# Two-block model: projection of block 2 by token tiles, one router for both tiles, softmax division on GpSimd, output stored in quarters

## What is computed

```python
def second_block(x, mem, g_mix, w_in, qk_gain, na_rpb, t5_table, g_mem, w_mem_kv, w_out, g_ffn, w_r1, b_r1, w_r2, b_r2, w1, w3, w2):
    ...
        x = x + jnp.concatenate([out_na, out_dil, out_mem], axis=-1) @ w_out[l]
        x = x + hierarchical_moe(rms_norm_2(x, g_ffn[l]), w_r1[l], b_r1[l], w_r2[l], b_r2[l], w1[l], w3[l], w2[l])

def hierarchical_moe(h, w_r1, b_r1, w_r2, b_r2, w1, w3, w2):
    ...
    grp_logits = (t @ w_r1).astype(jnp.float32) + b_r1.astype(jnp.float32)
    grp_prob = jax.nn.softmax(grp_logits, axis=-1)
    grp_idx = jnp.argmax(grp_logits, axis=-1)
    ...
    fine_logits = ((t @ w_r2).astype(jnp.float32) + b_r2.astype(jnp.float32)).reshape(n, N_GROUPS, EXPERTS_PER_GROUP)
    fine_sel = jnp.take_along_axis(fine_logits, grp_idx[:, None, None], axis=1)[:, 0]
    top_val, top_idx = lax.top_k(fine_sel, TOP_K)
    gate = grp_gate * jax.nn.softmax(top_val, axis=-1)
    ...
        a = jax.nn.silu(xb @ w1[e]) * (xb @ w3[e])
        return a @ w2[e]
```

## Time and profile before

| | us |
|---|---|
| runs of the kernel | 2553.66, 2555.37, 2559.77 (median 2555.37) |
| the profiled execution, whole | 2554.65 |
| its span in the profile | 2552.9 |
| PE / DVE / ACT / POOL busy | 2091.7 / 1346.4 / 846.9 / 622.0 |
| attention of block 2 | from 1945.8 to 2016.3 |
| output projection, norm, router | from 2016.4 to 2083.0 |
| rounds of experts | from 2083.0 to 2544.9 |
| output store | from 2546.5 to the end |

### The profile page before, as it was taken

The page is one execution under the profiler, slowest core; times in us unless marked ns, Lnnn a source line. Parts: engine busy times, 40 slices in busy tenths (PEclk is TensorE's granted clock), DMA queues, the critical chain, the costliest instruction groups (busy, mean ns, idle before and its releaser), DMA issues.

```text
span 2552.9 us, 24815 instructions
## 1 busy us (share of the span) xinstructions
PE 2091.7 (82%) x8226; PEld 1068.0 (42%) x8226; DVE 1346.4 (53%) x3202; ACT 846.9 (33%) x2245; POOL 622.0 (24%) x585
## 2 busy tenths in 40 slices
PE   5997978798799889799889779877999966666665
PEld 1554632354264455265456224322674532222221
DVE  2885887666647966646976577764106230111110
ACT  1214144344436644435734344443104210000000
POOL 1000044433334433333433444442101000000000
PEclk9997999999999999999999999999999978888888
DMA  8792799999999999999999999999540139999997
GB/s 331 296 372 89 296 374 421 421 421 420 394 421 421 388 417 421 421 397 421 365 410 422 421 421 418 414 421 418 197 160 34 67 147 428 427 429 428 428 429 325
DMA packets 107145, 915.96 MB, mean 359 GB/s; under 512 B 12406, under 2 KB 12692, under 8 KB 15572
## 3 DMA queue, kind: packets, MB, share of 16 engines
q0 software_dynamic: 76800, 549.70, 52.8%
q1 hardware_dynamic: 30228, 364.82, 34.5%
HBM read 913.37 MB, written 6.06 MB: 360 GB/s over the span
## 4 chain that ended last, share of the span: by engine, by line
PE 39%; DMA 36%; DVE 15%; ACT 6%; issue 3%; POOL 1%; SPq 0%; DVEq 0%; POOLq 0%; ACTq 0%
DMA arena<-in_peer_uv_dram,arena 18%; PE summed L1071 15%; DMA arena<-in_moe_pieces_dram 15%; PE gp L1143 5%; DVE y L2224 4%; PE gp L873 3%; DMA arena<-in_w_slots_dram 3%; PE gp L858 3%; DVE h L2026 2%; PE gp L1139 2%; PE gp L1404 2%; PE turned L958 1%; ACT arena L1652 1%; PE scores L944 1%; ACT L1646 1%
## 5 line engine op out<-in xcount | busy, mean ns | idle before, releaser
L1071 PE MATMUL summed<-arena 128*128 128x512 f32 x2048 | 993.5, 620 | 210.8 <-ACT arena L1652 187.6
L2224 DVE CUSTOM_DVE_ANT_0 y<-arena,h 128x1024 f32<-128x1024 f32 x512 | 627.2, 1225 | 398.7 <-DMA arena<-in_peer_uv_dram,arena 351.5
L804 POOL DMA_INDIRECT arena<-in_peer_uv_dram,arena x512 | 580.2, 1133 | 925.2 <-PE summed L1071 809.1
L1071 PEld LDWEIGHTS summed<-arena 128*128 128x128 f32 x2048 | 367.5, 193 | 749.1 <-ACT arena L1652 403.9
L1646 ACT ACTIVATE arena<-arena 128x1 f32<-128x1 f32 x512 | 102.8, 201 | 517.6 <-DVE arena L2224 517.0
L1404 PE MATMUL gp<-arena,mod 128*32 128x512 f32 x1024 | 161.2, 764 | 120.7 <-DMA arena<-in_moe_pieces_dram 119.5
L1652 ACT ACTIVATE arena<-cst,arena 128x128 f32<-128x128 f32 x512 | 205.8, 402 | 16.7
L2554 DVE TENSOR_TENSOR mod<-mod,gp 128x512 f32<-128x512 f32 x8 | 5.5, 689 | 385.4 <-ACT mod L1876 385.4
L1649 ACT ACTIVATE arena<-arena 128x1 f32<-128x1 f32 x512 | 151.1, 295 | 20.8 <-DVE arena L2213 4.1
L873 PE MATMUL gp<-hT,arena 128*128 128x256 f32 x608 | 135.6, 386 | 4.1 <-DMA arena<-in_w_slots_dram 3.3
L1404 PEld LDWEIGHTS gp<-arena,mod 128*32 128x32 f32 x1024 | 31.9, 125 | 245.0 <-DMA arena<-in_moe_pieces_dram 184.1
(11 more groups left out here) (399 smaller groups left out, 2033.7 us busy)
## 6 DMA issues: line engine op xcount, KB each, us to landing
arena<-in_moe_pieces_dram SPq DMA_DIRECT2D x96, 2048.0 KB, 25.7
arena<-in_w_slots_dram SPq DMA_DIRECT2D x47, 2048.0 KB, 10.0
mod<-in_w_parts_dram SPq DMA_DIRECT2D x29, 1024.0 KB, 9.3
arena<-in_w_parts_dram SPq DMA_DIRECT2D x29, 1024.0 KB
arena<-in_peer_uv_dram,arena POOLq DMA_INDIRECT x512
t_rep<-t_rows POOLq DMA_DIRECT2D x1, 3066.0 KB, 14.8
arena<-t_rep POOLq DMA_DIRECT2D x1, 2304.0 KB, 11.1
na_rep<-na_rows POOLq DMA_DIRECT2D x1, 1778.0 KB, 7.7
```

Of the source, the lines that this page charges most:

```text
L804: pool.indirect_dma_start(rowbuf[b], None, a["peer_uv"].rearrange("l n d -> (l n) d"), bass.IndirectOffsetOnAxis(ap=idx[:, col(n):col(n) + ...
L1071: mm = pe.matmul(op[:, b, :], diag[:, n % DIAGS, :], rowbuf[n % ROWS][:, D + b * 512:D + (b + 1) * 512], start=n % SLOTS == 0, stop=n % SL ...
L2224: v.tensor_tensor_reduce(y[:, t, :], rowbuf[n % ROWS][:, 0:D], h[:, t, :], 1.0, 0.0, ALU.mult, ALU.add, dots[:, c:c + 1]).then_inc(udot, 1)
```

## The change

POOL no longer builds diagonal matrices. It multiplies each segment's exponentials, in place, by the inverse sums (128x512 in block 2; in MoBA 128x128 and 128x256), and PE transposes them with the identity. PE now waits per segment, not per unit. The projection goes tile 0 of both slots, then tile 1. Residual, norm, transposition and router product are done per tile, and the filling multiplications are gone. The router treats both tiles in one instruction where it can; `r_done` is raised once `picked` is there, and the gates follow while PE makes the ranks. The count of overflowing tokens comes after the first `select`, and PE waits for `flag_ready` only after the first `up`. The last `scatter` uses four PSUM banks. Each quarter of `x` is stored when its last addition is done, ahead of the branch.

```diff
-        in_order += phase_slots["in2"] + phase_slots["out2"]
+        in_order += phase_slots["in2"]
         order += [(n, j) for n in in_order for j in range(len(slots[n][2]))]
+        order += [(n, t) for t in range(T) for n in phase_slots["out2"]]
...
+            for n in range(2 * T):
+                c = slice(n % 2 * CH, (n % 2 + 1) * CH)
+                sync.wait_ge(scat_read, 4 * (QUADS - 1) + n + 1)
+                sync.dma_start(out[0, n // 2 * P:(n // 2 + 1) * P, c], x[:, n // 2, c]).then_inc(out_done, 16)
             sync.wait_ge(flag_ready, 1)
...
+            def divide_rows(stage_name):
+
+                units, segs = att[stage_name]
+                u0 = unit_base[stage_name]
+                for i, sg in enumerate(segs):
+                    u = sg["u"]
+                    if sg["first"]:
+                        pool.wait_ge(d_inv, u0 + u + 1)
+                    inv = den[:, 2 * (u % 4):2 * (u % 4) + 2]
+                    if sg["keys"][0] == S:
+                        c0 = CH * (i % 6 % 3)
+                        rows = logits[stage_name][i % 6 // 3][:, c0:c0 + CH].rearrange("p (t n) -> p t n", t=T)
+                        pool.tensor_tensor(rows, rows, inv.unsqueeze(2).to_broadcast([P, T, S]), ALU.mult).then_inc(scale_ready, 1)
+                    else:
+                        for t in range(T):
+                            rows = logit(stage_name, sg, i, t)
+                            ins = pool.tensor_tensor(rows, rows, inv[:, t:t + 1].to_broadcast([P, sg["keys"][t]]), ALU.mult)
+                        ins.then_inc(scale_ready, 1)
...
-                    pe.wait_ge(scale_ready, u0 + sg["u"] + 1)
+                    pe.wait_ge(scale_ready, b0 + i + 1)
...
-                                mm = pe.matmul(tp[:, i % 2, c * S + t * P:c * S + (t + 1) * P],
-                                               logit(stage_name, sg, i, t)[:, c * P:(c + 1) * P], scale[:, t, :], start=True, stop=True)
+                                mm = pe.transpose(tp[:, i % 2, c * S + t * P:c * S + (t + 1) * P],
+                                                  logit(stage_name, sg, i, t)[:, c * P:(c + 1) * P], ident)
...
-            project("out2")
-            keep_clock("out2", 8)
-            turn_h(4)
-            hT_ready()
-
             for t in range(T):
+                project("out2", tile=t)
+            for t in range(T):
+                pe.wait_ge(h_ready, 4 * T + t + 1)
+                turn_rows(h[:, t, :])
+                hT_ready()
...
-            pe.wait_ge(flag_ready, 1)
...
             up(0)
+            pe.wait_ge(flag_ready, 1)
             turn_sel(0, False)
...
-            residual("out2", T * 5)
-            norm(4, x)
+            for t in range(T):
+                v.wait_ge(gemm_moved, group_of[phase_slots["out2"][-1], t] + 1)
+                v.tensor_tensor(x[:, t, :], x[:, t, :], y[:, t, :], ALU.add).then_inc(x_ready, 1)
+                v.wait_ge(x_ready, 4 * T + t + 1)
+                sum_of_squares(t)
+                last_norm(t)
```

More of the change, by code:

```diff
@@ L817, in _ @@
             load_gain(5, a["g_ffn_2"][0])
[L818 removed]
+            divide_rows("block2")
         @block.tensor
@@ L1853, in _ @@
             attention("block2")
-            move("out2")
-            norm(4)
-            move_turned()
+            move("out2", tile=0)
+            tile_root(4 + 2 * T)
+            move("out2", tile=1)
+            move_turned_rows(0)
+            tile_root(4 + 2 * T + 1)
+            move_turned_rows(1)
             act.wait_ge(r_pre, 1)
-            act.activation(route[:, 128:136], route[:, 128:136], ACT.Exp).then_inc(r_exp, 1)
-            act.wait_ge(r_pre, 2)
-            act.activation(route[:, 136:138], route[:, 136:138], ACT.Exp).then_inc(r_exp, 1)
+            act.activation(route[:, 128:138], route[:, 128:138], ACT.Exp).then_inc(r_exp, 1)
             def expert(e2, i):
@@ L1992, in attention @@
                             if u >= 4:
-                                v.wait_ge(scale_ready, u0 + u - 3)
+                                v.wait_ge(scale_ready, b0 + units[u - 4]["first"] + units[u - 4]["n"])
                             if stage_name == "moba":
@@ L2127, in rms_heads @@
                 link(v.reciprocal(small[:, c1:c1 + T * nh], small[:, c1:c1 + T * nh]))
-            def residual(name, n):
-                v.wait_ge(gemm_moved, last_group[name])
-                for t in range(T):
-                    v.tensor_tensor(x[:, t, :], x[:, t, :], y[:, t, :], ALU.add).then_inc(x_ready, 1)
-                v.wait_ge(x_ready, n)
             def first_residual(t):
@@ L2522, in _ @@
-            v.sem_inc(r_done, 1)
+                ins = v.max(gm[:, t, :], gl8[:, t, :])
+            link(ins)
+            for t in range(T):
+                ins = v.max_index(route_u[:, 8 * t:8 * t + 8], gm[:, t, :], gl8[:, t, :])
+            link(ins)
+            link(v.tensor_copy(gi.unsqueeze(2), route_u[:, 0:16].rearrange("p (t n) -> p t n", t=T)[:, :, 0:1]))
+            v.tensor_tensor(ge, gl8[:, :, 0:4], gm[:, :, 0:1].to_broadcast([P, T, 4]), ALU.subtract)
+            link(v.tensor_tensor(oh, iota[:, 0:4].unsqueeze(1).to_broadcast([P, T, 4]), gi.unsqueeze(2).to_broadcast([P, T, 4]), ALU.is_equal))
@@ new lines, in _ @@
+            for t in range(T):
+                ins = v.tensor_tensor(tmp[:, t], fine[:, t, :].rearrange("p (g n) -> p g n", g=N_GRP),
+                                      oh[:, t, :].unsqueeze(2).to_broadcast([P, N_GRP, PER_GRP]), ALU.mult)
+            link(ins)
+            link(v.tensor_reduce(fsel, tmp.rearrange("p t g n -> p t n g"), AX.X, ALU.add))
+            for t in range(T):
+                ins = v.max(fm[:, t, :], fsel[:, t, :])
+            link(ins)
+            v.tensor_tensor(p1.unsqueeze(2), fm[:, :, 1:2], fm[:, :, 0:1], ALU.subtract).then_inc(r_pre, 1)
@@ new lines, in _ @@
+            for t in range(T):
+                ins = v.max_index(route_u[:, 16 + 8 * t:24 + 8 * t], fm[:, t, :], fsel[:, t, :])
+            link(ins)
+            link(v.tensor_copy(fi, route_u[:, 16:32].rearrange("p (t n) -> p t n", t=T)[:, :, 0:2]))
+            for c, hot_c in ((0, hot0), (1, hot1)):
+                ins = v.tensor_tensor(hot_c, iota[:, 0:8].unsqueeze(1).to_broadcast(both), fi[:, :, c:c + 1].to_broadcast(both), ALU.is_equal)
+            link(ins)
+            link(v.tensor_tensor(fm, hot0, hot1, ALU.add))
@@ new lines, in _ @@
+            for t in range(T):
+                ins = v.tensor_tensor(picked[:, t, :].rearrange("p (g n) -> p g n", g=N_GRP),
+                                      oh[:, t, :].unsqueeze(2).to_broadcast([P, N_GRP, PER_GRP]),
+                                      fm[:, t, :].unsqueeze(1).to_broadcast([P, N_GRP, PER_GRP]), ALU.mult)
+            ins.then_inc(r_done, 1)
+            v.wait_ge(r_exp, 1)
+            link(v.tensor_reduce(gsum, ge, AX.X, ALU.add))
+            link(v.scalar_tensor_tensor(out=gg[:, :, 0], in0=p1, scalar=1.0, in1=gsum, op0=ALU.add, op1=ALU.mult))
@@ L2568, in _ @@
             select(0)
+            v.tensor_tensor(flat[4], flat[3], flat[6], ALU.subtract)
+            v.wait_ge(over_sum, 1)
+            v.tensor_copy(flag, tp[:, 1, 0:1]).then_inc(flag_ready, 1)
             take_up(0)
```

116 lines of the change are left out of this document (47 added, 69 removed).

## The result

The changed kernel takes **2531.42 us** (median of five runs, 2529.58 to 2537.81) against 2555.37 before (five runs, 2550.16 to 2559.77): ratio **0.9914, 95% interval 0.9898 to 0.993**, or 22 us less, 18 to 26 with the interval (the two medians are 24.0 us apart). Forecast were 2526.5 us in a range of 2518 to 2538. The time lies in the range, 4.9 us above the forecast; among the terms one has the wrong sign, which only the trace shows. The profiled execution took 2535.62 us, one of the longer ones.

What follows compares the result with a forecast made beforehand. The last stage is bound by transfers, so its first piece's use counts, reached through TensorE, then VectorE. Terms -7.5 - 1.0 - 7.4 - 8.1 - 4.2 = -28.2 us from 2554.65 led to 2526.5 us, range 2518 to 2538.

Steps and rivals of the forecast that it cites:

- One sign of being wrong: Last stage: forecast wrong if the stream of pieces does not start earlier by the sum of terms 1 to 4, 24 us.
- Term 1: Block 2's attention: pure transpositions replace TensorE's scaled products, with GpSimd's doubled product mostly hidden; -7.5 us.
- Term 3: Block 2's projection to router product: only tile 1's norm, transposition and half product remain behind the projection; -7.4 us.
- Term 4: Router: joint instructions for both tiles, gates hiding the ranks, cut-off and count off the path to selection; -8.1 us.
- Term 2: MoBA attention: transpositions save TensorE time, partly lost to waits for GpSimd, the gain handed on to the projection; -1.0 us.
- Rival B: Attention and projection of block 2: TensorE falls back to 1.2 GHz, whole kernel slower at 2583 us; chance 4%.
- Term 5: Kernel's end: last store asked for right at the last addition, and only a quarter left to transfer; -4.2 us.
- Rival A: Attention: GpSimd becomes the bound, at products of 1.5 us or more, eating all of term 1; 2534 us; chance 10%.
- Rival C: Half of terms 3 and 4 lost: joint instructions no cheaper than separate ones, ScalarE's copies delay tile 1; 2534 us; chance 8%.

Runs made afterwards that it cites:

- pool_twice: The changed kernel with GpSimd's work in block 2's attention doubled by a second, unused product ahead of each one; 2535.71 us, ratio 0.9933.
- block2_undone: The changed kernel with the division undone in block 2's attention alone, so the scaled products are back there; 2535.47 us, ratio 0.9924.

## Why the prediction was right, and where it was not

The total lies in the range, and the stages of block 2 did what the terms say. One sign of being wrong that the prediction had set itself did come, though: the stream was to start 24 us earlier and did so by 17.9. In the profiled pair terms 1, 3 and 4 gave 24.0 us where 23.0 stood, term 2 took 3.5 where it was to give 1.0, and 2.6 were lost in stretches that the change does not touch.

- **Term 1 (-7.5): right in its working, 1.6 us too large.** Up to the first wait for GpSimd in the dilated units the gain is 5.3 us (38.3 to 33.0) where 5.5 stood; behind it 1.1 us (32.25 to 31.2) where I kept 2.0. Over all profiles (without `pool_twice`) the stage goes from 70.8 to 64.9 us, -5.9. All but one of the nine profiles with the division there show a short fall of the clock between 1980 and 2010, none of the five with products does. Part of the missing 1.6 us is probably this: the six profiles with one such fall took 64.2 to 64.7 us, the two with two 66.5.
- **Term 2 (-1.0): wrong in sign.** The step that failed is the one that ended "What follows on this chain is a projection, so the gain is handed on". What was handed on was the lower clock, 2.4 of the +3.3 us. The gain itself did not come either: without an early fall of the clock MoBA attention took 21.84 us with the division (`block2_undone`) and 21.55 with products, with a short one (0.72 to 0.74 in 240 to 246) 23.6 to 24.3 against 22.9 to 23.0. How much of this is GpSimd's 0.98 us per segment where 0.62 stood, and how much the clock, was not separated. Rival B had the mechanism, at the wrong attention: it was priced in block 2, where the stage is long and TensorE busy, and not in MoBA, which has eight segments and ends in waits of 0.7 to 1.5 us.
- **Term 3 (-7.4): right.** 18.2 to 10.6 us in the profiled pair; over all profiles without fillers there 17.9 (three) to 10.9 (eight), -7.0. That the clock might fall before tile 1 is turned was in the 0.6 us allowed; it fell about then (0.74 in 2048 to 2052), and the product took 3.64 us, not 3.0.
- **Term 4 (-8.1): right in kind, undersized.** It is 10.0 us. The step is the price of a joint instruction: 24 at 0.22 gave 5.3 us, and took 4.0, as those without a wait between them follow closely (three of them took 0.38 us on the chain); the gates hid wholly behind the ranks (1.6 us, not 2.1).
- **Term 5 (-4.2): oversized.** It is 3.0 us on average. The 5.6 us wait of the earlier trace rows was a long one; with the same single store the other two profiles end 1.4 us sooner.
- **Sum.** Stages of all profiles: -5.9 + 3.3 - 7.0 - 10.0 - 3.0 = -22.6, measured -22.0 (-18 to -26). Against the forecast of -28.2, terms 1, 2, 3 and 5 lack 7.5 us together, and term 4 made good 1.9 of them. Without that error of opposite sign the sum would have missed by 7.5 us instead of 5.6.
- **Rival A** did not come: its point was a product of 1.5 us or more, and it is 1.04. **Rival C** neither: joint instructions were cheaper than forecast.

## What to carry to other kernels

Halving TensorE's work in a stage that already waits can lower its clock, and the bill comes in the dense stage behind it: ask of each edit that thins TensorE's work what runs right after, and look at the granted clock there in several profiles, not in one. Filling products paid here only when they were sized from the idle time in the trace and from their own measured duration; what is too much goes straight onto the chain, and more so where they run at the lower clock. Where the measured time scatters by several us, compare the lengths of stages over all profiles at hand: two totals here said "no difference" where a stage had changed by 3 us.

## What the runs showed of the hardware that I had not expected

- A nearly equal busy time just ahead did not bring an equal clock. In 246 to 252 us TensorE was busy 3.68 us before and 3.71 us after, and only after the change did the clock fall, to 0.50 from 252 on. The instructions differed: products before, transpositions after. But so did the six us ahead (busy 6.00 us at 1.00 before, 5.51 us at 0.72 after). The Trainium skill (TensorE: Matmul & The Clock Gate, Part 4) states that a transposition does not count as TensorE activity in the same way; these windows agree with it, but no run here held the instants of work equal and changed the kind alone, so it stays open whether the kind or the timing counted.
- Whether the last scatter ran at 1.00 or 0.50 of the clock was chance between executions with the same instructions (3.71 and 5.78 us in two profiles of the changed kernel): the fall came in both, and what differed was when.
- A float32 product shows as two records, a transposition as one: eight blocks took 1.98 us and 1.02 us on the chain at the same clock.
